# Chunk products of three linear-attention mixers: contraction over all 128 rows, with the other chunk's rows of the moving operand held at zero

## What is computed

```python
# RWKV-7, 8 heads of 64: state S, one token
sa = S @ a_t
S  = S * d_t + outer(sa, b_t) + outer(v_t, k_t);  y_t = S @ r_t
# GLA, 4 heads, key 64, value 128: one chunk
o = att @ v_c + (q_c * exp(b_c)) @ S
S = S * exp(b_end) + (k_c * exp(b_end - b_c)).T @ v_c
# gated delta rule (GDN), 4 heads, key 128, value 128: one chunk
v_new = u_c - w_c @ S
o = (q_c * exp(g_c)) @ S + att_c @ v_new
S = S * exp(g_end) + (k_c * exp(g_end - g_c)).T @ v_new
```

## Time and profile before

| | |
|---|---|
| median of three runs | 3624.35 us |
| profiled execution, own time | 3627.77 us |
| its span, first to last instruction | 3626.0 us |
| mean granted clock of TensorE | 0.921 of full speed |
| busy: PE, DVE, ACT | 91%, 51%, 18% of the span |
| HBM read | 426.42 MB, 118 GB/s over the span |

### The profile page before, as it was taken

The page is one execution under the profiler, slowest core; times in us unless marked ns, Lnnn a source line. Parts: engine busy times, 40 slices in busy tenths (PEclk is TensorE's granted clock), DMA queues, the critical chain, the costliest instruction groups (busy, mean ns, idle before and its releaser), DMA issues.

```text
span 3626.0 us, 50620 instructions
## 1 busy us (share of the span) xinstructions
PE 3295.8 (91%) x21614; PEld 2503.3 (69%) x21614; DVE 1844.4 (51%) x2775; ACT 658.7 (18%) x1254; POOL 38.0 (1%) x76
## 2 busy tenths in 40 slices
PE   8999978888998999987888997889999998997898
PEld 8986665455996997766454995445588885455697
DVE  5654343464655564244454654456433472278565
ACT  1111101211103102110220211235111101233110
POOL 1000000000000000000000000000000000000000
PEclk9999966889999999975789998989999999998899
DMA  7653301104745755310112653120122343221353
GB/s 251 227 200 117 128 2 64 68 32 133 253 152 184 255 193 180 128 56 1 70 71 93 221 197 133 50 70 1 47 86 78 104 159 115 93 93 47 122 167 113
DMA packets 279696, 430.74 MB, mean 119 GB/s; under 512 B 9880, under 2 KB 147456, under 8 KB 279472
## 3 DMA queue, kind: packets, MB, share of 16 engines
q1 hardware_dynamic: 273920, 411.52, 33.5%
q0 software_dynamic: 5088, 14.85, 1.2%
q10 hardware_dynamic: 464, 1.12, 0.1%
HBM read 426.42 MB, written 1.05 MB: 118 GB/s over the span
## 4 chain that ended last, share of the span: by engine, by line
PE 81%; DVE 13%; ACT 3%; issue 2%; DMA 0%; DVEq 0%; ACTq 0%
PE bank L438 79%; PE bank L441 2%; DVE arena L734 1%; DVE arena L2222 1%; ACT xT L2632 1%; DVE arena L3434 1%; ACT xT L983 1%; DVE arena L3355 1%; DVE arena L1675 0%; DVE arena L3469 0%; ACT arena L2936 0%; DVE arena L3060 0%; DVE stats L908 0%; DMA arena<-in_ln_b 0%; DVE ctok L1687 0%
## 5 line engine op out<-in xcount | busy, mean ns | idle before, releaser
L438 PE MATMUL bank<-arena 128*128 128x128 f32 (+6 forms) x7164 | 879.5, 302 | 69.2 <-DVE arena L1567 14.2
L438 PEld LDWEIGHTS bank<-arena 128*128 128x128 f32 (+2 forms) x7164 | 731.8, 179 | 214.2 <-issue 39.9
L438 PE MATMUL bank<-xT,ring 128*128 128x128 f32 (+2 forms) x4576 | 809.1, 337 | 17.8 <-ACTq L2640 10.0
L438 PEld LDWEIGHTS bank<-xT,ring 128*128 128x128 f32 x4576 | 680.0, 195 | 140.5 <-issue 73.0
L438 PE MATMUL bank<-ring,xT 128*128 128x512 f32 (+1 forms) x1344 | 578.9, 585 | 5.7 <-ACTq L1331 2.6
L438 PE MATMUL bank<-ring,arena 128*128 128x256 f32 (+1 forms) x1584 | 451.3, 439 | 25.4 <-ACTq L2450 11.8
L438 PEld LDWEIGHTS bank<-ring,xT 128*128 128x128 f32 x1344 | 249.2, 193 | 296.3 <-issue 289.4
L438 PEld LDWEIGHTS bank<-ring,arena 128*128 128x128 f32 x1584 | 305.3, 194 | 152.7 <-issue 90.3
L774 DVE TENSOR_TENSOR arena<-arena,bank 128x256 f32<-128x256 f32 (+1 forms) x198 | 92.1, 465 | 430.2 <-PE bank L438 289.9
L734 DVE TENSOR_TENSOR arena<-ring,arena 128x1024 f32<-128x1024 f32 (+1 forms) x216 | 257.1, 1190 | 7.4
L686 ACT COPY arena<-bank 128x256 f32<-128x256 f32 (+1 forms) x264 | 107.8, 408 | 779.7 <-PE bank L438 778.7
(11 more groups left out here) (386 smaller groups left out, 2229.8 us busy)
## 6 DMA issues: line engine op xcount, KB each, us to landing
ring<-in_ffn_w SPq DMA_DIRECT2D x88, 1024.0 KB, 7.9
ring<-in_w_in SPq DMA_DIRECT2D x32, 2048.0 KB, 7.7
ring<-in_ffn_w_in SPq DMA_DIRECT2D x44, 1024.0 KB, 7.7
arena<-in_ada_w SPq DMA_DIRECT2D x18, 2048.0 KB, 13.6
ring<-in_ffn_w SPq DMA_DIRECT2D x16, 2048.0 KB, 7.9
ring<-in_ffn_w_out SPq DMA_DIRECT2D x12, 2048.0 KB, 8.0
ring<-in_hgrn_w_in SPq DMA_DIRECT2D x12, 2048.0 KB, 7.9
ring<-in_ffn_w SPq DMA_DIRECT2D x8, 1536.0 KB, 6.7
```

Of the source, the lines that this page charges most:

```text
L438: return self.e.matmul(o, lhsT, rhs, start=start, stop=stop, skip_group_check=True)
```

## The change

Every product of the sequential parts that took 64 rows now takes all 128: the chunk matrices (`M4`, `Um`, `BKtok`, `gatt`, `gktok`, `dU`, `datt`, `dk_tok`) are read with both chunks' rows, and the moving operand is a tile whose rows of the other chunk are zero, one such tile for each chunk. The number of products, their columns and the banks stay. The columns of the chunk matrices stay 64 (128 for `dk_tok`).

The zeros and the values are written by ACT. `act_clear` writes 64 rows x 512 columns of zeros; `act_own_values` copies 64 rows x 512 of `v_tok`. A layer has six clears in `act_mix` behind a wait on `rwkv_T_ready`, two clears and four copies in `act_rwkv` behind a wait on `v_tok_ready`, four clears and four copies at the start of `act_gla`, and four clears in `act_gdn` before the solve. PE waits for `own_values_ready` behind each RWKV solve and ahead of the GLA chunks, and for `own_rows_clear` behind the GDN solve. DVE writes `Xs`, `SAs`, `dX` and `dvn` at the rows of the chunk as before, into the tile of that chunk. No DMA changes.

```diff
-        Xs = brT[:].rearrange("p k t -> p (k t)")[:, 0:512]
-        SAs = brT[:].rearrange("p k t -> p (k t)")[:, 512:1024]
+        x_homes = [brT[:].rearrange("p k t -> p (k t)"), sq[:].rearrange("p k t -> p (k t)")]
+        Xs = [x[:, 0:512] for x in x_homes]
+        SAs = [x[:, 512:1024] for x in x_homes]
+        v_flat = eiL[:].rearrange("p k t -> p (k t)")
+        v_own = [[v_flat[:, 512 * c:512 * c + 512] for c in range(2)], [ctok[:, c, 512:1024] for c in range(2)]]
...
+            act.wait_ge(rwkv_T_ready, act.due(rwkv_T_ready))
+            for c in range(2):
+                for tt in range(2):
+                    act_clear(act, v_own[tt][c], c)
+            act_clear(act, Xs[0], 0)
+            act_clear(act, SAs[0], 0)
...
         def act_rwkv(act):
+            act.wait_ge(v_tok_ready, act.due(v_tok_ready))
+            act_clear(act, Xs[1], 1)
+            act_clear(act, SAs[1], 1)
             for tt in range(2):
+                act_own_values(act, tt)
                 act_solve(act, Pm)
                 act_head_std(act)
+
+        def act_clear(act, x, c):
+            other = CHUNKS[1 - c]
+            ins = act.e.activation(x[other].rearrange("p (a n) -> p a n", n=P),
+                                   ones[other].unsqueeze(1).broadcast_to([C, 4, P]), ACT.Copy, scale=0.0)
...
+        def act_own_values(act, tt):
+            for c, r_ in enumerate(CHUNKS):
+                ins = act.e.copy(v_own[tt][c][r_], v_tok[r_, tt])
...
-                    v.tensor_copy(Xs[r_], bank[r_, :]).then_inc(to_dve.freed, dve.up(to_dve.freed))
+                    v.tensor_copy(Xs[c][r_], bank[r_, :]).then_inc(to_dve.freed, dve.up(to_dve.freed))
...
                 pe_solve(pe, Tm, Um, Am, Pm)
+                pe.wait_ge(own_values_ready, pe.due(own_values_ready, 2))
...
                         pe.mm(o, AR[:, par, hp, ct], Hst[:, hp], True, False)
-                        mm = pe.mm(o, M4[r_, h, 0], v_tok[r_, tt, h * 64:(h + 1) * 64], False, True)
+                        mm = pe.mm(o, M4[:, h, 0], v_own[tt][c][:, h * 64:(h + 1) * 64], False, True)
...
-                        mm = pe.mm(bank[r_, h * 64:(h + 1) * 64], Um[r_, h], Xs[r_, h * 64:(h + 1) * 64])
+                        mm = pe.mm(bank[r_, h * 64:(h + 1) * 64], Um[:, h], Xs[c][:, h * 64:(h + 1) * 64])
...
-                        pe.mm(o, M4[r_, h, 1], v_tok[r_, tt, h * 64:(h + 1) * 64], False, False)
-                        mm = pe.mm(o, M4[r_, h, 3], SAs[r_, h * 64:(h + 1) * 64], False, True)
+                        pe.mm(o, M4[:, h, 1], v_own[tt][c][:, h * 64:(h + 1) * 64], False, False)
+                        mm = pe.mm(o, M4[:, h, 3], SAs[c][:, h * 64:(h + 1) * 64], False, True)
...
-                        pe.mm(o, BKtok[r_, 0, h * 64:(h + 1) * 64], SAs[r_, h * 64:(h + 1) * 64], True, False)
+                        pe.mm(o, BKtok[:, 0, h * 64:(h + 1) * 64], SAs[c][:, h * 64:(h + 1) * 64], True, False)
...
+            for tt in range(2):
+                for c, r_ in enumerate(CHUNKS):
+                    act_clear(act, gv_own[tt][c], c)
+                    ins = act.e.copy(gv_own[tt][c][r_], gla_v[r_, tt])
...
-                        pe.mm(o, gatt[r_, par, 2 * tt + hp], gla_v[r_, tt, h * P:(h + 1) * P], True, False)
+                        pe.mm(o, gatt[:, par, 2 * tt + hp], gv_own[tt][c][:, h * P:(h + 1) * P], True, False)
                         mm = pe.mm(o, gQb[:, par, o0:o0 + 64], gS[:, hp], False, True)
...
-                        mm = pe.mm(bank[...], gktok[r_, tt, h * 64:(h + 1) * 64], gla_v[r_, tt, h * P:(h + 1) * P])
+                        mm = pe.mm(bank[...], gktok[:, tt, h * 64:(h + 1) * 64], gv_own[tt][c][:, h * P:(h + 1) * P])
...
+            for c in range(2):
+                act_clear(act, dX[c], c)
+                act_clear(act, dvn[c], c)
+            act.sem_inc(own_rows_clear, act.up(own_rows_clear))
...
-                        mm = pe.mm(bank[r_, h * P:(h + 1) * P], dU[r_, 4 * tt + h], dX[r_, h * P:(h + 1) * P])
+                        mm = pe.mm(bank[r_, h * P:(h + 1) * P], dU[:, 4 * tt + h], dX[c][:, h * P:(h + 1) * P])
...
-                        mm = pe.mm(bank[r_, h * P:(h + 1) * P], datt[r_, tt, h], dvn[r_, h * P:(h + 1) * P])
+                        mm = pe.mm(bank[r_, h * P:(h + 1) * P], datt[:, tt, h], dvn[c][:, h * P:(h + 1) * P])
...
-                        mm = pe.mm(bank[:, s_], dk_tok[r_, tt, s_], dX[r_, s_])
+                        mm = pe.mm(bank[:, s_], dk_tok[:, tt, s_], dX[c][:, s_])
```

More of the change, by code:

```diff
@@ L185, in two_blocks @@
         gdn_gate_ready = sem("gdn_gate_ready")
+        own_values_ready = sem("own_values_ready")
+        own_rows_clear = sem("own_rows_clear")
         gk_abs_ready = sem("gk_abs_ready")
@@ L1441, in act_rwkv @@
         def act_rwkv(act):
+            act.wait_ge(v_tok_ready, act.due(v_tok_ready))
+            act_clear(act, Xs[1], 1)
+            act_clear(act, SAs[1], 1)
             for tt in range(2):
+                act_own_values(act, tt)
                 act_solve(act, Pm)
                 act_head_std(act)
+        def act_clear(act, x, c):
+            other = CHUNKS[1 - c]
+            ins = act.e.activation(x[other].rearrange("p (a n) -> p a n", n=P),
+                                   ones[other].unsqueeze(1).broadcast_to([C, 4, P]), ACT.Copy, scale=0.0)
+            ins.then_inc(act_step, act.up(act_step))
+            act.wait_ge(act_step, act.sent(act_step))
+        def act_own_values(act, tt):
+            for c, r_ in enumerate(CHUNKS):
+                ins = act.e.copy(v_own[tt][c][r_], v_tok[r_, tt])
+                ins.then_inc(own_values_ready, act.up(own_values_ready))
+                act.wait_ge(own_values_ready, act.sent(own_values_ready))
         def act_head_std(act):
@@ L1591, in dve_rwkv @@
                     bank = to_dve.filled_bank()
-                    v.tensor_copy(SAs[r_], bank[r_, :]).then_inc(to_dve.freed, dve.up(to_dve.freed))
+                    v.tensor_copy(SAs[c][r_], bank[r_, :]).then_inc(to_dve.freed, dve.up(to_dve.freed))
                     dve.wait_ge(to_dve.freed, dve.sent(to_dve.freed))
@@ L1825, in pe_rwkv @@
                         o = bank[64 * par:64 * par + 64, hp * 64:(hp + 1) * 64]
-                        pe.mm(o, BKtok[r_, 0, h * 64:(h + 1) * 64], SAs[r_, h * 64:(h + 1) * 64], True, False)
-                        mm = pe.mm(o, BKtok[r_, 1, h * 64:(h + 1) * 64],
-                                   v_tok[r_, tt, h * 64:(h + 1) * 64], False, True)
+                        pe.mm(o, BKtok[:, 0, h * 64:(h + 1) * 64], SAs[c][:, h * 64:(h + 1) * 64], True, False)
+                        mm = pe.mm(o, BKtok[:, 1, h * 64:(h + 1) * 64],
+                                   v_own[tt][c][:, h * 64:(h + 1) * 64], False, True)
                         if h == 7:
@@ L1855, in two_blocks @@
         gtmp2 = g(512)
+        gv_own = [[g(512) for _ in range(2)] for _ in range(2)]
         def act_gla(act):
+            for tt in range(2):
+                for c, r_ in enumerate(CHUNKS):
+                    act_clear(act, gv_own[tt][c], c)
+                    ins = act.e.copy(gv_own[tt][c][r_], gla_v[r_, tt])
+                    ins.then_inc(own_values_ready, act.up(own_values_ready))
+                    act.wait_ge(own_values_ready, act.sent(own_values_ready))
             act.wait_ge(gk_abs_ready, act.due(gk_abs_ready))
@@ L2039, in pe_gla @@
                                     mm.then_inc(to_dve.filled, 1)
+            pe.wait_ge(own_values_ready, pe.due(own_values_ready, 4))
             for tt in range(2):
@@ L2057, in pe_gla @@
                         hp, par = h // 2, h % 2
-                        mm = pe.mm(bank[64 * par:64 * par + 64, hp * P:(hp + 1) * P], gktok[r_, tt, h * 64:(h + 1) * 64],
-                                   gla_v[r_, tt, h * P:(h + 1) * P])
+                        mm = pe.mm(bank[64 * par:64 * par + 64, hp * P:(hp + 1) * P], gktok[:, tt, h * 64:(h + 1) * 64],
+                                   gv_own[tt][c][:, h * P:(h + 1) * P])
                         if h == 3:
@@ L2081, in two_blocks @@
         dU = d(8, C)
-        dX = at(WORK + 8 * SEQ, 512)
-        dvn = at(WORK + 8 * SEQ + 512, 512)
+        dX = [at(WORK + 512 * c, 512) for c in range(2)]
+        dvn = [at(WORK + 512 * c, 512) for c in range(2, 4)]
         z_s, sp_s, g_s = dsm[:, 0:8], dsm[:, 8:16], dsm[:, 16:24]
@@ L2366, in pe_gdn @@
             pe_solve(pe, dT, dU, dAm, dPm)
+            pe.wait_ge(own_rows_clear, pe.due(own_rows_clear))
             blk = pe.block()
```

6 lines of the change are left out of this document (3 added, 3 removed).

## The result

The changed kernel takes 3524.17 us (median of 4 runs, 3523.60 to 3525.91) against 3624.89 us before (4 runs, 3622.24 to 3627.48): a ratio of 0.9723, interval 0.9706 to 0.9740, 100.7 us saved. The forecast was 3526 us. The profiled execution took 3525.91 us, its span is 3524.1 us, and its mean granted clock is 0.950 where it was 0.921.

A forecast was written before the change was run, and what follows sets the result against it. PE bounds the kernel (busy 91%, 81% of the chain), taking turns with DVE. Savings 83.7 - 5.6 + 18.2 + 2 = 98.3 us, from 3624.35 to 3526 us; low end 3510, high end 3570.

The forecast's parts named there:

- Pauses: RWKV stages A and C: 15 changes between 128 and 64 rows cost 2.81 and 2.7 us, and would vanish.
- no pause from operands: Rival: the pause comes from alternating two operands or tiles, so A and C keep their length; 3624 us, chance 0.03.
- Which clock: RWKV chunks: full clock saves 83.7 us, half clock 45.2; full taken. Most chunks full 0.70; half, mixed or slow slots 0.22.
- a comparison with the solve alone: The solve fills all rows and keeps clock 1.00 though PE idles more there, so the new RWKV stages should too.
- idle gaps of 0.84 us would leave the clock up: RWKV chunks: idle gaps of 0.84 to 1.05 us between stages were taken not to lower the clock.
- a whole chunk of eight at half clock: One of eight RWKV chunks falls back to half clock, 15.74 instead of 10.13 us: 5.6 us returned.
- Slots: RWKV: an instruction of 128 rows and 64 columns takes 0.060 us at full clock, 0.110 at half.
- weights of 128 rows cannot be loaded behind the product: Rival: in a single strip every instruction waits for its load; loses from 0.165 us a slot; 3661 us, chance 0.05.
- RWKV: Eight chunks go from 164.7 to 81.0 us at full clock, 83.7 saved, less 5.6 for one at half clock.
- GLA: GLA chunks save 1.9, 3.65, 0.95 and 2.6 us: 9.1 us a layer, 18.2 for both.
- the lower of my bounds: Fourth GLA chunk, clock open after PE idles 3.6 us: 1.45 to 3.65 us saved, 2.6 taken.
- GDN: Pace unchanged, but fuller rows may hold the clock up: 2 us saved, bounds 0 and 4.3.

The follow-up runs named there:

- sorting: Kernel before, 64 rows kept, but in RWKV stages A and C and GLA all state products come before the chunk-matrix products: 3560.94 us, ratio 0.9819.
- the bursts: Separate kernel computing nothing of the reference: six unbroken bursts of 240 products, differing in rows, strips, columns or operands; one run, 722.39 us.
- short groups of 128 rows: In the separate 722.39 us timing kernel: sixteen groups of 8 products with 128 rows, a DVE copy between groups.
- the kernel with RWKV alone: Kernel before with only the RWKV products taking 128 rows, GLA and GDN unchanged: 3548.43 us, ratio 0.9788.
- the kernel with 16 products ahead of the solve: Changed kernel plus unread 512-column products in PE's idle stretches: 16 before the second tile's solve, others before branch projections and fourth GLA chunk: 3537.67 us.
- long groups: In the separate 722.39 us timing kernel: sixteen groups of 24 products, with 64 or with 128 rows, a DVE copy between groups.

## Why the prediction was right, and where its terms were off

*Pauses.* Predicted: 0.18 to 0.19 us at each change between 128 and 64 rows, 2.8 us in stage A. Shown by sorting (A 3.86 at half clock with one change left) and by the bursts (0.202 against 0.107 us an instruction, and no pause from operands).

*Which clock.* The weakest step, a comparison with the solve alone, held: 1.00 over the tiles of chunks, with one slip in a layer. The comparison named the right quantity, the rows: the bursts of 64 and of 128 rows differ in nothing else, and in the sorted kernel, where the pauses were gone and the 64 rows stayed, five of eight stages C ran at half clock. That idle gaps of 0.84 us would leave the clock up was the guess in it, and in part luck: short groups of 128 rows lost the clock over such gaps, long ones kept it. The slips were over-sized: I had a whole chunk of eight at half clock, 5.6 us; it was two stages C, 2 x 1.55 = 3.1 us. The stage that slips is always the C of a tile's first chunk, but the tile varies: the second in both layers here, layer 0's first in the kernel with RWKV alone (5.55 us at 471.7), all four in the kernel with 16 products ahead of the solve. Why is open. So is what exactly makes the clock fall.

*Slots.* 0.060 us for 64 columns over 128 rows: (2.08 - 0.20) / 32 = 0.059, and in long groups (3.01 - 0.20) / 48 = 0.0585. The rival "weights of 128 rows cannot be loaded behind the product" needed 0.165 (0.159, had it counted the 0.6 us of starts that it adds in its own sum) and falls.

*RWKV.* 81.7 us against 78.1: 2.5 of the difference are the smaller slips, the rest the slots.

*GLA.* 15.1 us against 18.2, mis-sized in two terms. The timeline of TensorE, the fourth chunk:

```profile
620.39 4.53 PE L440 MATMUL bank<-arena 128*64 128x128 f32 x24 [3.70 <-DVEq L2018]
```

It ran at half clock after 3.70 us of idle time: 1.5 saved where I took 2.6, the lower of my bounds, 1.1 a layer. And the chain of waits at the second chunk has a member that I had not counted:

```profile
610.73 1.98 PE bank L440 x19
612.73 0.71 DVE arena L2004
613.46 0.36 DVE arena L2010
613.84 0.36 DVE arena L2010
```

PE is on it for only 19 of its 24 instructions; then DVE's copy of the output (0.69 us) decides, which used to lie hidden beside the state products of a 6.05 us stage. PE's idle time between chunks grew from 0.97 to 1.16 us. Two hand-overs make 0.4 us a layer; with the 1.1 that is 1.5 a layer, the 3.1 us that are missing.

*GDN.* 2.7 us against 2. Layer 0's second tile went from 19.85 to 16.49 us as the higher clock promised. Layer 1's, which had been quick (15.6 us), went to 16.46 and gave 0.7 back. Both now stand at the same clock (0.91), so what was gained is layer 0's lost clock, not a faster product.

*Elsewhere.* 2.4 us came from stretches that the change doesn't touch, between 1.7 more and 2.5 less each. The likely source is the phase in which the clock enters them; no run here isolates it.

*The total.* That 3526 came within 2 us of 3524.17 is in part luck: against the profiled spans RWKV gave 3.6 us more than forecast, GLA 3.1 less, GDN 0.7 more, and 2.4 came from elsewhere.

## What to carry to other kernels

When TensorE is busy and its granted clock is still 0.50, look at the rows of its products before looking at its gaps: here zeros that fill the other half of the rows cost nothing in pace and brought the clock from 0.54 to 1.00, and where they cannot be had, sorting products of one shape together removes a pause at every change (0.19 us at half clock), but does not hold the clock. What such a change is worth is found by pricing each stage at both clocks and then asking, chunk by chunk, what the engine did just before. A stage that becomes short enough brings the neighbour's copy onto the chain, so the saving is to be cut at the next engine's own leg.

## What the runs showed of the hardware that I had not expected

- 102.66 us of unbroken products with 64 rows and all 128 columns left the clock at 0.50, while 64-row products in two strips finished 480 instructions in 16.00 us. So more columns in use did not bring the clock up, though that burst also moves its columns at half the rate of the others.
- Once up, the clock outlasts stages that could not have raised it: stage X with 64 rows changed nothing (3525.36 us), and in the sorted kernel one tile of four, with three quarters of its products on 64 rows, stayed at 1.00. In the other three it fell and stayed down to the end of the tile.
- Products that nobody reads, 0.88 us each, can be worth their place where PE waits anyway: 14.3 us in this kernel, 22 with one more in each gap of RWKV, and 13.5 us lost when the first were twice as many.
